# Query weights laid out by head, key weights turned on the host, and sixteen modulation tiles in another stage of a hybrid decoder step

## What is computed

```python
def adaln(c, w, b):                      # six shift/scale/gate vectors for each layer
    m = jax.nn.silu(c) @ w + b
    m = m.reshape(c.shape[0], 1, 6, D_MODEL)
    return [m[:, :, k] for k in range(6)]

def mla_project(h, q_off, w_in, q_g, kv_g, w_qb):
    ...
    q = (cq @ w_qb).reshape(b, l, MLA_HEADS, QK_NOPE + QK_ROPE)
    q_nope = q[..., :QK_NOPE]
    q_pe = rope(q[..., QK_NOPE:], pos)
    return q_nope, q_pe, ckv, kr

def mla_prompt(h, w_in, q_g, kv_g, w_qb, w_kvb, w_o):
    ...
    o = causal_attention(q, k, kv[..., QK_NOPE:], 0)
    return o.reshape(b, l, MLA_HEADS * V_DIM) @ w_o, ckv, kr

def mla_sample(h, past_lat, past_rope, w_in, q_g, kv_g, w_qb, w_kvb, w_o):
    ...
    q_lat = jnp.einsum('bshd,rhd->bshr', q_nope, w[..., :QK_NOPE])
    k_lat = jnp.concatenate([past_lat, ckv], axis=1)      # 1024 cached tokens from pages
    ...

def swiglu(h, wg, wu, wd):
    return (jax.nn.silu(h @ wg) * (h @ wu)) @ wd
```

## Time and profile before

| | us |
|---|---|
| median of 3 runs | 1569.45 (1568.14 to 1572.27) |
| the profiled execution | 1570.95 |
| its span | 1569.3 |
| heads, first query product to last modulation tile | 76.7 to 154.2 |
| prompt attention, first scores to the samples' first scores | 157.9 to 222.3 |
| samples' scores and values | 222.3 to 258.7 |
| output product and norm | 258.7 to 298.7 |
| gate and up products | 298.7 to 455.6 |
| down products | 456.3 to 537.5 |

### The profile page before, as it was taken

The page is one execution under the profiler, slowest core; times in us unless marked ns, Lnnn a source line. Parts: engine busy times, 40 slices in busy tenths (PEclk is TensorE's granted clock), DMA queues, the critical chain, the costliest instruction groups (busy, mean ns, idle before and its releaser), DMA issues.

```text
span 1569.3 us, 24319 instructions
## 1 busy us (share of the span) xinstructions
PE 1497.1 (95%) x9928; PEld 886.5 (56%) x9928; DVE 370.2 (24%) x903; ACT 258.8 (16%) x586; POOL 117.0 (7%) x175
## 2 busy tenths in 40 slices
PE   6999988999999999999998999999999999998998
PEld 3544556788888788688785554543344233432342
DVE  2223432300000255545476100010000101011104
ACT  2122321200000122377303100000000000000001
POOL 1101651000000100100011100000000100010000
PEclk9999999999999999999999999999999999999999
DMA  9759989343334734562478899999999999999996
GB/s 380 309 215 383 364 237 338 133 164 134 128 113 138 244 118 158 152 256 82 153 272 315 286 358 388 394 405 405 419 417 420 405 420 399 420 403 419 418 418 225
DMA packets 100172, 463.23 MB, mean 295 GB/s; under 512 B 12014, under 2 KB 31243, under 8 KB 58421
## 3 DMA queue, kind: packets, MB, share of 16 engines
q1 hardware_dynamic: 86912, 419.44, 68.9%
q0 software_dynamic: 10640, 41.03, 7.7%
q10 hardware_dynamic: 2512, 1.23, 0.3%
HBM read 446.30 MB, written 15.55 MB: 294 GB/s over the span
## 4 chain that ended last, share of the span: by engine, by line
PE 80%; DMA 12%; DVE 5%; issue 1%; SPq 1%; ACT 1%; POOL 0%; DVEq 0%
PE bank L1625 11%; PE bank L1180 10%; PE bank L1150 9%; PE bank L1675 6%; PE bank L1194 5%; PE bank L1518 5%; DMA ringx<-in_moe_w_up 4%; DMA ring<-in_moe_w_up 3%; PE bank L1637 3%; PE bank L1228 3%; PE bank L892 3%; PE bank L1533 2%; PE bank L1559 2%; PE bank L926 2%; DMA ring<-in_w_ada 2%; PE bank L979 2%
## 5 line engine op out<-in xcount | busy, mean ns | idle before, releaser
L1625 PE MATMUL bank<-ring,hg 128*32 128x512 f32 (+1 forms) x1456 | 206.9, 566 | 11.6 <-DMA ring<-in_moe_w_up 8.6
L1180 PE MATMUL bank<-hT,ring 128*128 128x264 f32 x704 | 156.9, 386 | 0.3 <-ACT hT L1728 0.3
L1180 PEld LDWEIGHTS bank<-hT,ring 128*128 128x128 f32 x704 | 133.7, 190 | 23.4 <-issue 0.6
L1625 PE MATMUL bank<-ringx,hg 128*32 128x512 f32 (+1 forms) x848 | 145.5, 567 | 0.9 <-DMA ring<-in_moe_w_up 0.9
L1625 PEld LDWEIGHTS bank<-ring,hg 128*32 128x32 f32 x1456 | 63.5, 111 | 113.5 <-issue 102.1
L1150 PE MATMUL bank<-hT,ring 128*128 128x264 f32 x512 | 118.3, 393 | 1.6 <-ACT hT L1728 1.3
L1150 PEld LDWEIGHTS bank<-hT,ring 128*128 128x128 f32 x512 | 98.9, 194 | 19.9 <-issue 2.1
L1675 PE MATMUL bank<-ring,turnH 128*32 128x512 f32 x768 | 93.7, 609 | 0.0
L1194 PE MATMUL bank<-actT,ring 128*128 128x264 f32 x352 | 79.1, 386 | 0.6 <-DVE actT L2214 0.6
L1518 PE MATMUL bank<-ring,hg 128*128 128x512 f32 (+1 forms) x192 | 78.0, 560 | 0.6 <-ACT hg L1943 0.6
L1625 PEld LDWEIGHTS bank<-ringx,hg 128*32 128x32 f32 x848 | 42.6, 112 | 58.3 <-issue 55.9
(11 more groups left out here) (569 smaller groups left out, 1798.1 us busy)
## 6 DMA issues: line engine op xcount, KB each, us to landing
ring<-in_moe_w_down SPq DMA_DIRECT2D x53, 1024.0 KB, 16.9
ring<-in_w_ada SPq DMA_DIRECT2D x48, 1024.0 KB, 11.0
ring<-in_moe_w_up SPq DMA_DIRECT2D x40, 1024.0 KB, 16.7
ring<-in_moe_w_gate SPq DMA_DIRECT2D x32, 1024.0 KB
ringx<-in_moe_w_gate SPq DMA_DIRECT2D x27, 1024.0 KB, 12.0
ringx<-in_moe_w_down SPq DMA_DIRECT2D x24, 1024.0 KB, 17.4
ring<-in_ssm_w_in SPq DMA_DIRECT2D x20, 1024.0 KB, 4.8
ringx<-in_moe_w_up SPq DMA_DIRECT2D x19, 1024.0 KB, 15.3
```

The costliest lines, as they stand in the source:

```text
L1180: m = mm(bank[2 * w + q][:, 0:T], slot8(tl)[:, k, q * P:(q + 1) * P], hT[:, k, :], start=k == 0, stop=k == DC - 1)
L1625: m = mm(bank[2 * b_ + u][rows, 0:HALVES[g][u]], hg[:, k, rows], w[:, kk, 512 * u:512 * u + HALVES[g][u]], start=k == 0, stop=k == DC - 1, ...
```

## The change

- The query weights are packed on the host: each head has 128 columns instead of 96, the extra 32 being the rotary columns with their halves exchanged. Even heads lie as (plain 64, rotary 32, exchanged 32), odd heads as (rotary, exchanged, plain). The query product then gives the exchanged half by itself, the product with the rotation matrix (L962) is gone, and DVE does the rotary arithmetic straight from PSUM. Keys of odd heads lie in the same way; unused rows are set to zero by DVE at the start, and the rotary keys are copied in later, behind the copies of `ltok`.
- The key weights come turned from the host (`wkT`, 1 MB, a transfer of POOL); the transposes (L992) and ACT's copies of them are gone. The sample queries are formed for two heads at a time, one on partitions 0 to 63 and one on 64 to 127.
- Because `wqb` now fills three of the four parts of `latcache`, POOL's early load of one sample's turned pages is gone; all four samples' pages are loaded from the end of the heads stage on.
- Sixteen modulation tiles of layer 1, and two of their three turns, leave the prompt attention and stand in pairs behind the gate and up products of steps 1 to 8 of the dense layer.
- SP fills the output weights behind the turned pages, ahead of the token pages. The gate and up fills are written out in a new order with the sixteen tiles among them, and loops of ACT, DVE and SP are unrolled.
- The eight small gate products stand behind the first down step instead of in the norm; `keep_clock` there runs four matmuls instead of two.

The diff, cut to its core:

```diff
-ADA0, IN0, ADAR, ADA1, LAT, WO = 0, 8, 11, 27, 51, 55
-GU, DOWN = 59, 81
+ADA0, IN0, ADAR, ADA1, LAT, WO = 0, 8, 11, 27, 35, 39
+GU, DOWN = 43, 81
+def ffn_order():
+    order = []
+    for j in range(FC // 2):
+        order += [("gate_up", 2 * j), ("gate_up", 2 * j + 1)]
+        if 1 <= j <= DC:
+            order += [("ada", 2 * j - 2), ("ada", 2 * j - 1)]
+    return order
...
# SP
-        ada(1, ADA1, 0, 3)
+        ada(1, ADA1, 0, 1)
...
+        for j in range(4):
+            fill8(WO + j, 256, wo_d[:, j, :])
         sp.wait_ge(s["samp_scored"], 3)
         for b in range(4, NB - 1):
             for n in range(NPG):
                 load_tokens(sp, sample_pages, b, n).then_inc(lat_ready[b], 16)
-        for j in range(4):
-            fill8(WO + j, 256, wo_d[:, j, :])
...
# POOL
+        g.dma_start(wkT, a["mla_wk_turned"].rearrange("p (h r) -> p h r", h=H // 2)).then_inc(s["wkt_in"], 16)
...
-        turned(2)
-        g.wait_ge(s["wk_turned"], H)
+        g.wait_ge(s["k_done"], H // 2)
+        turned(3)
         g.wait_ge(s["q_done"], H)
         turned(0)
         turned(1)
-        turned(3)
+        turned(2)
...
# PE, heads
-            mm(bank[4][64:96, 0:T], cst[64:96, C_ROT:C_ROT + ROPE], qT[64:96, h, :], start=True, stop=True).then_inc(s["q_rotated"], 1)
-            pe.wait_ge(s["wk_copied"], h + 1)
             for c in range(KC):
-                q0 = (c * H + h) * NB
-                m = mm(bank[7][:, q0:q0 + NB], wkT[:, h % 2, c * P:(c + 1) * P], qT[0:NOPE, h, TP:T], start=True, stop=True)
+                for u in range(2):
+                    rows, q0 = slice(64 * u, 64 * u + 64), (c * (H // 2) + pair) * NB
+                    m = mm(bank[(7, 6)[u]][:, q0:q0 + NB], wkT[rows, pair, c * P:(c + 1) * P], qT[rows, 2 * pair + u, TP:T], start=True, stop=True)
...
-            for c in range(KC):
-                m = pe.transpose(bank[6][0:NOPE, c * P:(c + 1) * P], wkvb[:, c, h * P:h * P + NOPE], ident)
-            m.then_inc(s["wk_turned"], 1)
...
# PE, prompt attention
-            ada_tile(ADA1 + t, t % DC, bank[(3, 7, 3)[t // DC]])
-            if t % DC == 1:
-                ada1_turn(t // DC - 1)
+            if h == 1:
+                ada_turn(3, bank[2][:, 0:144])
             turn_p(h)
...
# PE, dense layer
-        keep_clock(bank[5], 2)
-        for c in range(DC):
-            m = mm(bank[4 + c // 4][0:9, (c % 4) * P:(c % 4 + 1) * P], mod[:, 1, 5 * DC + c, :], ident, start=True, stop=True)
-        m.then_inc(s["gates_copied"], 1)
+        keep_clock(bank[5], 4)
...
         for j in range(FC // 2):
-            gate_up(j % 4, j // 4)
+            gate_up(j)
+            if 1 <= j <= DC:
+                for i in (2 * j - 2, 2 * j - 1):
+                    ada_tile(FFN_AT["ada", i], i % DC, bank[4 + i // DC])
+            if j in (6, 10):
+                blk = (6, 10).index(j)
+                ada_turn(4 + blk, bank[6][:, 144 * blk:144 * (blk + 1)])
...
+            if j == 0:
+                pe.wait_ge(s["ada_added"], 5)
+                for c in range(DC):
+                    m = mm(bank[4 + c // 4][0:9, (c % 4) * P:(c % 4 + 1) * P], mod[:, 1, 5 * DC + c, :], ident, start=True, stop=True)
+                m.then_inc(s["gates_copied"], 1)
...
# DVE
+        v.memset(qT[32:64, 1::2, :], 0.0)
+        v.memset(kT[32:64, 1::2, :], 0.0).then_inc(s["kt_zeroed"], 1)
...
-        v.tensor_copy(kT[64:96, :, :], mid(krT[64:96, 1, 0:TP], H)).then_inc(s["lora_vector"], 1)
...
+        v.tensor_copy(kT[0:32, 1::2, :], mid(krT[0:32, 0, 0:TP], H // 2))
+        v.tensor_copy(kT[64:96, 0::2, :], mid(krT[64:96, 1, 0:TP], H // 2)).then_inc(s["kt_rope"], 1)
...
         for j in range(4):
-            v.tensor_copy(qpeT[32 * j:32 * j + 32, :, 0:H], qT[64:96, :, TP + j:T:4].rearrange("p h u -> p u h"))
+            for u, r0 in ((0, 64), (1, 0)):
+                v.tensor_copy(qpeT[32 * j:32 * j + 32, :, u:H:2], qT[r0:r0 + 32, u::2, TP + j:T:4].rearrange("p h u -> p u h"))
```

169 lines of the change are left out of this document (90 added, 79 removed).

## The result

The changed kernel takes 1577.45 us in the median of 20 runs (1567.36 to 1587.37) where the kernel before takes 1569.42 in 20 runs beside it (1565.27 to 1575.79): a ratio of 1.0047, 95% interval 1.0029 to 1.0065. It is slower by half a percent, and the interval leaves no change out. I forecast 1556.5. The profiled execution took 1578.06 us, its span is 1576.4.

The account below looks back on a forecast made before the run. PE was taken to bound heads and dense layer, and the attention with holes in it. Heads -12.9, attention -20.1, samples 0 and dense layer +20.1 sum to -12.9 us: 1556.5 from a median of 1569.45, range 1547 to 1566.

Parts of the forecast that it names:

- The dense layer (+20.1): Dense layer: sixteen added tiles in pairs 16.2 us, two turns 2.0, gate products out of the norm 1.9; together +20.1 us.
- Heads (-12.9): Heads stage: 13.4 us less PE work, 0.5 less ahead of it, 1.0 more DVE work behind the last tile; -12.9 us.
- the first rival: Heads stage: sample products of two heads run side by side, eight pairs take 4.3 us less, total 1552; chance 0.15.
- the one that costed the tiles' transfers at nothing: Heads stage: 1.8 MB more and 1 MB less moved, costed at 0 because DMA has 0.28 free; otherwise 2.8 us.
- Attention (-20.1): Prompt attention: fourteen heads go from 52.2 to 34.1 us (-18.1), another tile and turn go behind them (-2.0); -20.1 us.
- the term for the holes: Prompt attention: unexplained waits in PE's row, 7.1 us before, taken as 4 after, bounded by 0 and 7.1.
- What the tiles gave, they had to repay: Attention and dense layer: moved tiles cost in the dense layer what they gave in the attention, -20.1 against +20.1 us.
- The stages behind (0): Stages behind the dense layer: the forecast's sum has no term for them, so no change.
- holes stay or grow, or the clock drops: Prompt attention, with more idle time on PE: 5 to 9 us more, total 1561 to 1566; chance 0.12.
- The wait for instructions that the prediction named: Prompt attention: holes may be sequencers' instruction fetches through DMA queues; if mostly hidden, holes 0 and total 4 us lower.

## Why the prediction was wrong

1. **The dense layer (+20.1) was right**: +19.3.
2. **Heads (-12.9): -10.8.** The removed head work came, and the price of the first rival on top; seven pairs at 0.55 instead of 1.08 are 3.7 us, so -16.6 was there to be had. The step that failed is the one that costed the tiles' transfers at nothing, on a stage average (0.72 of DMA's share); I had named 2.8 us as the price if it fails. At the stage's end PE waits 0.6 and 2.9 us for tiles, and the products behind the second wait run at half clock (1.93 and 0.96 us instead of 0.99 and 0.55), 4.9 us in all. Most of the other 0.9 lies ahead of the stage, which began 0.4 us later instead of 0.5 earlier. What makes the tiles late is not isolated: they have 12 us less in which to come, and GpSimd's pages come into the queues at 132. On the chip without holes the wait of 2.9 us is the same; the scores began at 144.8 there, mostly because the stage itself began 1.3 us sooner.
3. **Attention (-20.1): -9.8.** This is the main failure, and the step is the term for the holes. I counted 7.1 us of PE's holes before, took 4 for after, and bounded them by 7.1. The chain of the changed kernel has 12.7 us in two. The bound was wrong because I took PE's idle time for the size of the holes. PE had tiles to run in part of them, which need no softmax; ACT waited 17.1 us. What the holes cost lies between the two, and above my bound: 13.3 us in the changed kernel (54.7 against 41.4 without holes), 8 to 9.5 in the kernel before (point 4). That includes the half clock behind each hole, which I did not cost at all. I also took it as chance where the holes fall; they fall where GpSimd's gathers run. The work itself was sized 1.0 us too low: without holes the attention takes 41.4 us, I had 44.4 with 4 of holes in it.
4. **What the tiles gave, they had to repay, as forecast, but not one for one.** Of the 64.5 us before, 8 to 9.5 were holes (55.0 with plain transfers; 56.3 with tiles on the chip that has none; both from other chips than the 64.5). So taking the tiles out gives 10 us with holes and 15 without, and putting them into the dense layer costs 19.
5. **The stages behind (0): +9.0.** I costed everything behind the dense layer at nothing since its code is the same, and this step failed too. The half clock in the token gather and the expert products is 8.2 us, the mixer 2.8, and the router's own products gave 1.7 back (3.73 us instead of 5.42). The mixer's 2.8 us come from its end. Its last vector work waits for state transfers; these are the pieces of the chain, before and then after:

```profile
811.75 15.17 DMA st<-in_state_ssm
```
```profile
811.19 16.09 DMA st<-in_state_ssm
```

and PE's first product behind that work, in order of time, before and then after:

```profile
833.27 0.71 PE L863 MATMUL bank<-hT,cst 128*128 128x264 f32 x2 [0.93 <-ACT hT L1718]
```
```profile
833.63 0.71 PE L877 MATMUL bank<-hT,cst 128*128 128x264 f32 x2 [3.21 <-ACT hT L1730]
```

   The transfers take 0.9 us more (and those before them 8.43 instead of 7.06), PE waits 3.2 us instead of 0.9, and behind the wait it has the granted clock 0.50 from 836 to 839 us. In the kernel before that stretch is at 1.00, and the half clock comes later, in the router's products (0.51 from 841 to 843). This is no chance: in all fourteen profiles with the head change the last state transfers take 16.0 to 16.5 us and PE waits 2.9 to 3.5, in all six without it 14.9 to 15.2 and 0.8 to 1.1. Of the ten profiles with the head change and the usual two keepers, nine have these wholly at half clock (3.78 us), and in seven of them the token gather stays there; in the five without the head change the keepers take 1.98 to 3.68 us and the token gather 8.3 to 8.6. So the head change seems to lead there by way of the mixer's wait. No run changed that wait alone, and why the state transfers take longer is open.
6. The first result came from one chip. On the chip without holes the sum came out: the profiled run of 1554.68 us lies 1.8 us from the forecast. That is luck in two ways. It is the fastest run of twelve, and the median there, 0.9993 of the kernel before (0.9977 to 1.0009), is no gain: the other eleven runs took 6 to 13 us longer at a lower clock, and by the other traces of that chip the kernel before has no holes to lose there either. And errors cancelled: the wait for tiles took back what the paired sample products gave, and the attention was 3 us shorter than forecast.

The rival "holes stay or grow, or the clock drops" is the case that came, with both halves at once. I gave it 0.12 and 5 to 9 us; it cost 8.7 in the attention beyond what I had allowed, and 8.2 in a stage that I had not costed. I found no version that beats both kernels on a chip with holes.

Left open: by what path the gathers stop PE, and why one chip of those seen doesn't show it. The trace of the changed kernel shows only that ACT starts its copy at 168.08, while the transposes that it waits for end by their records at 160.16. The wait for instructions that the prediction named is not what the holes look like: in the first the queues carry one instruction packet, landed before 163 us, while ACT stands until 168.08; in the second, from 176.6 to 180.5, there is none.

## What to carry to other kernels

Before you take independent work out of a stage, size its waits on the engines that wait, not on the one that was kept busy: the filler hides them only on that engine. See what runs on the other queues when such a wait falls, and move that once as a test before you build on the gap. And look for the half clock behind a change, also in stages whose code is the same: a stage of small products that begins at half clock may not climb out of it by itself; here it didn't in seven of nine profiles.

## What was not expected of the hardware

- GpSimd's indirect gathers (64 KB each, issued every 1.25 us) beside the attention go with stops of PE, ACT and DVE of 3 to 9 us, and lengthen the scores by 8 to 9 us for eight gathers. The changed kernel showed it in its first profile and in three series of runs on three chips, and on the chip of one series none of four kernels with gathers did.
- The 48 products of the token gather ran at half clock throughout (14.70 us, PE busy all the time) in seven of nine profiles in which the four keeper records ahead of them had done so too (3.78 us); in the other two they took 8.65 and 8.79 us. With eight keeper records ahead they ran at full clock in 8.26 us in all five profiles that have them.
- State transfers far behind a change took about 1 us longer in every one of fourteen profiles with it than in the six without, in code that is the same.
- Four small products of two heads, on different halves of the array's rows, take 0.55 us, as long as two on one half (0.54).
